# Forgetting bias of odd heads moved to rows 64 to 127 of the array

## The chip, the cores and the metric

The kernel runs on one core of a Trainium2 chip. The metric is the device time of one execution in microseconds (us), the median of several runs.

## What is computed

Two requests go through a hybrid encoder of two layers: a prompt of 256 tokens and a sample step of 32 tokens with 512 cached keys. A layer is a SwiGLU block, one wide projection that feeds three groups of heads (forgetting attention, RWKV-7, retention), an output projection, a second SwiGLU block and a gated embedding. The change concerns the forgetting attention, 8 heads of width 64. Cut to what matters:

```
def fox_block(q, k, v, cq, ck, mask):
    s = jnp.einsum('bqhd,bkhd->bhqk', q, k).astype(F32) * (HEAD_DIM ** -0.5)
    s = s + jnp.swapaxes(cq, 1, 2)[:, :, :, None] - jnp.swapaxes(ck, 1, 2)[:, :, None, :]
    s = jnp.where(mask[None, None], s, -jnp.inf)
    p = jax.nn.softmax(s, axis=-1).astype(v.dtype)
    return jnp.einsum('bhqk,bkhd->bqhd', p, v)
```

Here `cq` and `ck` are running sums of the log forget gates `logf`, per head and token. For the prompt the function is called once for each half of the 256 queries, for the sample with all 512 + 32 keys.

## The kernel before

Everything is written by hand for each engine, with semaphores between them; each engine runs its own instructions in the order of the code. Tokens lie along the free dimension (256 of the prompt, then 32 of the sample), features along the partitions. Two neighbouring heads 2p and 2p+1 form a pair: the even head's 64 features are partitions 0 to 63 of block p of `zT`, the odd head's are partitions 64 to 127.

The bias is made by TensorE. `foxL` (stationary side, 8 heads x 256 prompt columns, then 2 x 128 sample columns) and `foxR` (moving side, 256 + 512 + 32 columns) are all zeros but for rows 0 to 7 and 32 to 39, one row for each head. Rows 0 to 7 of `foxR` are ones and those of `foxL` the query sums; rows 32 to 39 of `foxR` are the key sums and those of `foxL` constants. A product over all 128 rows thus adds the bias to the scores in PSUM, and the query-key product over 64 rows is accumulated on top of it.

The rows are filled during the projection (`z_block` on TensorE, L1486; `z_next` on VectorE, which evicts a block, L931, and makes the low part of the next weights, L922): three scans L1049, L1050, L1052, a copy into `foxR` L1054, then L1056 and L1059 into `foxL`. The rest was zeroed or loaded once at the start (L354, L358 to L361).

The attention itself, once in each layer, is a chain between engines. On TensorE: `scores(0)` between the two calls of `head_sums` (L1752), then in a loop over p `scores(p + 1)`, the transposes of the softmax of pair p (L1804) and the products with the values (L1812). In `scores`, L1776 is the bias, four matmuls with 128, 256, 128 and 256 columns, and L1781 the query-key product, four matmuls with the same columns. VectorE takes the maximum (L1217) and divides by the sum (L1239 to L1241), ScalarE takes exp (L705) and copies the transposes (L712), VectorE gates the output (L1232). GpSimd meanwhile finishes the RWKV output (L460 to L466). Then comes the sample: bias L1823 (512 and 32 columns, twice), scores L1829 (64 rows x 32 columns of the array each), on VectorE the maximum and the softmax (L1278 to L1287), with L1265 and L1272 of the output projection among them, transposes L1840 and L1842, products with the cached values L1848 and L1850, and the output projection L1866.

An fp32 matmul stands in the trace as two records.

Of the kernel before, what the change touches and what calls it, by code (L numbers as in the profile page):

```python
# [79 lines left out]
for _name, _n in (("n1", DB), ("nm", DB), ("n2", DB), ("pn", DB), ("mu", 7), ("prev", 7), ("bf", 1), ("w0", 2),  # L80
# [22 lines left out]
    rsd=10, ro_ps=6, ro_ok=6, rgate=2, fu_ok=1, fl_ok=1, lgf_ok=1, fc_ok=3, vt_ps=3, vtc=3, fs_ps=8, fmx=16,  # L103
# [20 lines left out]
def program(nc, wcol, x_in, p_in, consts_in, params_in, foxl_in, kc_in, vc_in, clf_in, srwkv_in, sret_in,  # L124
            nf_in, y_out, k_out, v_out, logf_out, shift_out, rwkv_out, ret_out):
    with ExitStack() as ctx:
# [210 lines left out]
        with nc.Block() as block:  # L337
            @block.sync
            def _(sp):
# [14 lines left out]
                sp.dma_start(foxL[32:40, :], foxl_in).then_inc(start_sem, 16)  # L354

            @block.gpsimd
            def _(pool):
                pool.memset(foxL[:], 0.0).then_inc(clear_sem, 1)  # L358
                pool.memset(foxR[:], 0.0).then_inc(clear_sem, 1)
                pool.wait_ge(clear_sem, 2)  # L360
                pool.memset(foxR[0:8, :], 1.0).then_inc(clear_sem, 1)  # L361
# [10 lines left out]
        with nc.Block() as block:  # L372
# [100 lines left out]
            def _(act):  # L473
                n_chain = [0]
                for layer in range(DEPTH):
# [87 lines left out]
                    if layer == 0:  # L563
                        act.wait_ge(start_sem, 64)
# [239 lines left out]
            def _(dve):  # L804
                n_chain = [0]
                for layer in range(DEPTH):
# [106 lines left out]
                    if layer == 0:  # L913
                        dve.wait_ge(start_sem, 64)
# [126 lines left out]
                    for b in range(2):  # L1041
# [12 lines left out]
                    link(dve.tensor_copy(foxR[32:40, :], cbuf[e8, :]))  # L1054
                    z_next(22)
                    dve.tensor_tensor(foxLp[e8], cbuf[e8, 0:TP].unsqueeze(1).to_broadcast([8, FOX_H, TP]),  # L1056
                                      w.unsqueeze(2).to_broadcast([8, FOX_H, TP]), ALU.mult).then_inc(S["fc_ok"], 1)
                    for g in range(2):
                        dve.tensor_tensor(foxLs[e8, 128 * g:128 * g + 128].rearrange("p (b t) -> p b t", b=4),  # L1059
                                          cbuf[e8, TP + PAST:].unsqueeze(1).to_broadcast([8, 4, TS]),  # L1060
                                          w.rearrange("p (b g) -> p g b", g=2)[:, g, :].unsqueeze(2).to_broadcast([8, 4, TS]),
                                          ALU.mult).then_inc(S["fc_ok"], 1)
# [300 lines left out]
            def _(pe):  # L1363
                for layer in range(DEPTH):
# [107 lines left out]
                    if layer == 0:  # L1472
                        pe.wait_ge(start_sem, 64)
# [293 lines left out]
                    pe.wait_ge(S["fc_ok"], past["fc_ok"] + 3)  # L1767

                    def scores(p):
# [357 lines left out]
```

## Time and profile before

| | |
|---|---|
| median of 3 runs | 1533.01 us (1532.35 to 1534.19) |
| profiled execution | 1533.06 us, span 1531.2 us |
| granted TensorE clock over the span | 0.944 |
| TensorE matmul busy | 1445.7 us (94%) |
| VectorE busy | 936.0 us (61%) |
| ScalarE busy | 597.0 us (39%) |

Time outside the span is 1.9 us. The span is that from the first to the last instruction. A granted clock of 1.00 is 2.4 GHz and 0.50 is 1.2 GHz; times within a layer are given as us from the start of the span.

### The profile page before, as it was taken

To read this page: it belongs to the slowest core of one execution; us is meant where nothing else is said; L and a number is where in the kernel's file an instruction comes from. 1 tells how busy PE (TensorE), PEld (TensorE's weight loads), DVE (VectorE), ACT (ScalarE), POOL (GpSimd) and SP (SyncE) were. 2 spreads that over 40 slices of the span, in tenths; PEclk is the share of its full clock that TensorE was granted. 3 is DMA by queue.
4 is the path that set the end of the run, shared out by engine and by line. 5 is a ranking of instruction groups with operands and counts; after the bars stand their busy time and mean duration, and the time that the engine had idled before them with its cause. 6 is when DMAs were issued, how large, how long until landed. Compare 5 with 4: busy or idle time off the path is not lost.

```text
span 1531.2 us, 26488 instructions
## 1 busy us (share of the span) xinstructions
PE 1445.7 (94%) x11102; PEld 1381.5 (90%) x11102; DVE 936.0 (61%) x1517; ACT 597.0 (39%) x837; POOL 41.4 (3%) x67
## 2 busy tenths in 40 slices
PE   6999998997987999999999999999899789999997
PEld 6999998997766999999989999989787579999997
DVE  5666456867555566663766663579583645666536
ACT  5444343531133544432554442444210435444334
POOL 1000000001020000000000000000100200000000
PEclk9999999998676999999999999999985879999998
DMA  8444443340020444444444444343400123444440
GB/s 322 166 164 165 165 164 110 135 170 32 5 71 30 164 153 165 162 166 162 159 164 163 164 164 164 122 147 138 158 1 12 64 83 138 167 165 164 165 163 32
DMA packets 31318, 205.47 MB, mean 134 GB/s; under 512 B 4312, under 2 KB 5864, under 8 KB 7544
## 3 DMA queue, kind: packets, MB, share of 16 engines
q1 hardware_dynamic: 28672, 195.98, 35.3%
q0 software_dynamic: 2560, 8.26, 1.5%
q8 instruction: 64, 1.05, 0.3%
q14 instruction: 22, 0.18, 0.0%
HBM read 200.13 MB, written 4.10 MB: 133 GB/s over the span
## 4 chain that ended last, share of the span: by engine, by line
PE 87%; DVE 7%; ACT 3%; issue 2%; DMA 0%; SPq 0%; DVEq 0%; ACTq 0%
PE bank L1411 37%; PE bank L1434 18%; PE bank L1486 10%; PE bank L1903 3%; PE bank L1866 3%; PE bank L1594 1%; PE bank L1601 1%; PE bank L1871 1%; PE bank L1848 1%; PE bank L1884 1%; PE bank L1606 1%; PE bank L1687 1%; PE bank L1582 1%; PE bank L1717 1%; PE bank L1776 1%
## 5 line engine op out<-in xcount | busy, mean ns | idle before, releaser
L1411 PE MATMUL bank<-split_x,split_w 128*128 128x288 f32 x4224 | 569.4, 297 | 16.2 <-ACT split_x L498 11.8
L1411 PEld LDWEIGHTS bank<-split_x,split_w 128*128 128x128 f32 x4224 | 566.2, 189 | 18.9 <-issue 11.8
L831 DVE TENSOR_TENSOR split_w<-wc,split_w 128x2048 fp32r<-128x2048 f32 x139 | 318.6, 2292 | 343.4 <-ACT split_w L514 343.4
L514 ACT ACTIVATE split_w<-wc 128x2048 fp32r<-128x2048 f32 x139 | 266.4, 1916 | 397.7 <-PE bank L1411 206.2
L1434 PE MATMUL bank<-split_x,split_w 128*128 (+1 forms) x2112 | 282.3, 295 | 0.0
L1434 PEld LDWEIGHTS bank<-split_x,split_w 128*128 128x128 f32 x2112 | 281.8, 188 | 0.0
L1486 PE MATMUL bank<-split_h,split_x 128*128 128x288 f32 x752 | 115.5, 301 | 5.6 <-ACT split_x L572 4.2
L1486 PEld LDWEIGHTS bank<-split_h,split_x 128*128 128x128 f32 x752 | 105.7, 191 | 9.0 <-DVE zT L931 5.1
L572 ACT ACTIVATE split_x<-wc 128x1024 fp32r<-128x1024 f32 x62 | 65.2, 1057 | 112.2 <-PE bank L1486 96.7
L539 ACT ACTIVATE et<-hT 128x288 f32<-128x288 f32 x88 | 35.5, 445 | 110.3 <-DVE hT L850 110.3
L1486 PE MATMUL bank<-split_x 128*128 128x288 f32 x496 | 76.1, 296 | 0.0
L1486 PEld LDWEIGHTS bank<-split_x 128*128 128x128 f32 x496 | 69.5, 189 | 0.0
L1903 PE MATMUL bank<-split_x,split_w 128*128 128x288 f32 x384 | 52.9, 297 | 0.0
L1903 PEld LDWEIGHTS bank<-split_x,split_w 128*128 128x128 f32 x384 | 51.7, 189 | 1.1 <-ACT split_x L771 1.1
L931 DVE TENSOR_TENSOR zT<-bank,rs 128x288 f32<-128x288 f32 x62 | 28.1, 453 | 32.0 <-PE bank L1486 23.1
L1486 PE MATMUL bank<-split_h,split_e 128*128 128x288 f32 x240 | 39.2, 308 | 7.5 <-DVE split_e L922 7.5
L855 DVE SCALAR_TENSOR_TENSOR et<-et,hT 128x288 f32<-128x288 f32 x88 | 36.4, 455 | 12.7 <-ACT et L539 9.1
L922 DVE TENSOR_TENSOR split_x<-wc,split_x 128x1024 fp32r<-128x1024 f32 x32 | 39.0, 1218 | 7.8 <-ACT split_x L572 7.8
L1486 PEld LDWEIGHTS bank<-split_h,split_e 128*128 128x128 f32 x240 | 35.2, 198 | 8.4 <-DVE split_e L922 8.4
L861 DVE SCALAR_TENSOR_TENSOR et<-et,bank 128x288 f32<-128x288 f32 x88 | 39.3, 450 | 4.1 <-PE bank L1411 2.5
L922 DVE TENSOR_TENSOR split_e<-wc,split_x 128x1024 fp32r<-128x1024 f32 x30 | 36.5, 1217 | 6.8 <-ACT split_x L572 6.8
L850 DVE TENSOR_TENSOR hT<-bank,rs 128x288 f32<-128x288 f32 x88 | 35.9, 450 | 5.9 <-ACT rs L493 5.9
(293 smaller groups left out, 1404.7 us busy)
## 6 DMA issues: line engine op xcount, KB each, us to landing
wc<-wcol SPq DMA_DIRECT2D x182, 1024.0 KB, 4.8
con<-consts_in SPq DMA_DIRECT2D x1, 2182.0 KB
arena<-kc_in POOLq DMA_DIRECT2D x8, 256.0 KB, 3.3
arena<-vc_in POOLq DMA_DIRECT2D x2, 1024.0 KB, 5.2
xT<-x_in SPq DMA_DIRECT2D x2, 576.0 KB, 4.3
k_out<-zT POOLq DMA_DIRECT2D x8, 144.0 KB, 2.2
v_out<-zT POOLq DMA_DIRECT2D x8, 144.0 KB, 2.2
y_out<-hT SPq DMA_DIRECT2D x8, 144.0 KB, 1.9
```

Source lines behind the costliest of these rows:

```text
L514: act.activation(ws[(s + 1 - f) % 2][0], wc[:, p % RING, :], ACT.Copy).then_inc(S["cast"], 1)
L572: act.activation(zw[n % 2][0], z_raw(n), ACT.Copy).then_inc(S["zcast"], 1)
L831: dve.tensor_tensor(lo, wc[:, (POS_FFN[f] + s) % RING, :], hi, ALU.subtract).then_inc(S["wlo"], 1)
L850: dve.tensor_tensor(half[:, q % 2, :], bank[2 * (q % 4)][:, 0:T], rs[:], ALU.mult)\
L855: dve.scalar_tensor_tensor(e, e, 1.0, half[:, q % 2, :], ALU.add, ALU.mult)\
L861: dve.scalar_tensor_tensor(e, e, 0.5, bank[2 * (q % 4) + 1][:, 0:T], ALU.mult, ALU.mult)\
L922: dve.tensor_tensor(lo, z_raw(n), hi, ALU.subtract).then_inc(S["zlo"], 1)
L1411: mm = pe.matmul(o, w[:, k, cs], x[:, k, :], start=(n == 0 and k == 0), stop=(n == 2 and k == DB - 1))
L1434: return pe.matmul(bank[m][:, 0:T], w[:, kk, m * 128:m * 128 + 128], rhs, start=start, stop=stop)
L1486: mm = pe.matmul(o, w[:, k, :], zh_lo(k) if second else zh_hi[:, k, :], start=(i == 0 and k == 0), stop=(i == 2 and k == DB - 1))
L1866: pe.matmul(bank[2 * s + cc][:, 0:T], hi[:, k, cc * 128:cc * 128 + 128], x[:, k, :], start=(x is oh_hi and k == 4), stop=False)
L1903: mm = pe.matmul(bank[2 * s + cc][:, 0:T], w[:, k, cc * 128:cc * 128 + 128], x[:, k, :], start=(n == 0 and k == 0), stop=(n == 2 and k == ...
```

## The change

The even heads' biases stay in rows 0 to 7 and 32 to 39, and a second set is written in rows 64 to 71 and 96 to 103. `foxL` gets the query sums of even heads in rows 0 to 7 alone, those of odd heads in rows 64 to 71. A bias matmul now reads 64 rows, those of its own head's half, and the bias matmuls of a pair alternate between the halves, as the score matmuls already do. The constants are loaded twice, the ones are set twice, the copy into `foxR` is made twice, and the one multiply of 8 heads becomes two of 4 heads.

```
@@ first block
-                sp.dma_start(foxL[32:40, :], foxl_in).then_inc(start_sem, 16)
+                for row in (32, 96):
+                    sp.dma_start(foxL[row:row + 8, :], foxl_in).then_inc(start_sem, 16)
-                pool.memset(foxR[0:8, :], 1.0).then_inc(clear_sem, 1)
+                for row in (0, 64):
+                    pool.memset(foxR[row:row + 8, :], 1.0).then_inc(clear_sem, 1)
@@ VectorE, during the projection
-                    link(dve.tensor_copy(foxR[32:40, :], cbuf[e8, :]))
+                    for row in (32, 96):
+                        link(dve.tensor_copy(foxR[row:row + 8, :], cbuf[e8, :]))
                     z_next(22)
-                    dve.tensor_tensor(foxLp[e8], cbuf[e8, 0:TP].unsqueeze(1).to_broadcast([8, FOX_H, TP]),
-                                      w.unsqueeze(2).to_broadcast([8, FOX_H, TP]), ALU.mult).then_inc(S["fc_ok"], 1)
                     for g in range(2):
-                        dve.tensor_tensor(foxLs[e8, 128 * g:128 * g + 128].rearrange("p (b t) -> p b t", b=4),
+                        own = slice(64 * g, 64 * g + 8)
+                        mine = w.rearrange("p (b g) -> p g b", g=2)[:, g, :].unsqueeze(2)
+                        dve.tensor_tensor(foxLp[own].rearrange("p (b g) t -> p g b t", g=2)[:, g],
+                                          cbuf[e8, 0:TP].unsqueeze(1).to_broadcast([8, 4, TP]),
+                                          mine.to_broadcast([8, 4, TP]), ALU.mult).then_inc(S["fc_ok"], 1)
+                        dve.tensor_tensor(foxLs[own, 128 * g:128 * g + 128].rearrange("p (b t) -> p b t", b=4),
                                           cbuf[e8, TP + PAST:].unsqueeze(1).to_broadcast([8, 4, TS]),
@@ TensorE, scores
-                        for e in range(2):
-                            for q, k1, at in parts:
-                                pe.matmul(bank[score_bank(2 * p + e)][:, at:at + k1], foxLp[:, 2 * p + e, q:q + 128], foxR[:, 0:k1],
+                        for q, k1, at in parts:
+                            for e in range(2):
+                                hs = slice(64 * e, 64 * e + 64)
+                                pe.matmul(bank[score_bank(2 * p + e)][:, at:at + k1], foxLp[hs, 2 * p + e, q:q + 128], foxR[hs, 0:k1],
                                           start=(at == 0), stop=False, skip_group_check=True)
@@ TensorE, sample
-                    for g in range(2):
-                        for i, (k0, k1) in enumerate(keys):
-                            pe.matmul(bank[2 * g + i][:, 0:k1 - k0], foxLs[:, 128 * g:128 * g + 128], foxR[:, TP + k0:TP + k1],
+                    for i, (k0, k1) in enumerate(keys):
+                        for g in range(2):
+                            hs = slice(64 * g, 64 * g + 64)
+                            pe.matmul(bank[2 * g + i][:, 0:k1 - k0], foxLs[hs, 128 * g:128 * g + 128], foxR[hs, TP + k0:TP + k1],
                                       start=True, stop=False, skip_group_check=True)
```

The waits on `start_sem` and `fc_ok` count the added load (80 for 64) and the added multiply (4 for 3).

On TensorE, `scores(0)` of the first layer stands before as follows (the width is that of output rows x columns, and bank0 and bank1 are the two heads of pair 0):

```order
L1776 MATMUL bank0<-foxR,foxL 128x128
L1776 MATMUL bank0<-foxR,foxL 128x256
L1776 MATMUL bank1<-foxR,foxL 128x128
L1776 MATMUL bank1<-foxR,foxL 128x256
L1781 MATMUL bank0<-zT 128x128
L1781 MATMUL bank1<-zT 128x128
```

and with the change as follows (L1776 is now L1782, L1781 is L1787):

```order
L1782 MATMUL bank0<-foxR,foxL 128x128
L1782 MATMUL bank1<-foxR,foxL 128x128
L1782 MATMUL bank0<-foxR,foxL 128x256
L1782 MATMUL bank1<-foxR,foxL 128x256
L1787 MATMUL bank0<-zT 128x128
L1787 MATMUL bank1<-zT 128x128
```

The number and size of the matmuls are the same; banks 0 and 1 now alternate in the bias too.

On VectorE, the place in the projection where the rows are filled stands before as follows:

```order
L1054 COPY foxR<-extra 8x800
L931 TENSOR_TENSOR zT<-bank,rs 128x288
L922 TENSOR_TENSOR split_x<-wc,split_x 128x1024
L1056 TENSOR_TENSOR foxL<-extra,con 8x2048
L1059 TENSOR_TENSOR foxL<-extra,con 8x128 x2
L931 TENSOR_TENSOR zT<-bank,rs 128x288
```

and with the change as follows (L931 is now L933, L922 is L924):

```order
L1057 COPY foxR<-extra 8x800 x2
L933 TENSOR_TENSOR zT<-bank,rs 128x288
L924 TENSOR_TENSOR split_x<-wc,split_x 128x1024
L1062 TENSOR_TENSOR foxL<-extra,con 8x4x256
L1065 TENSOR_TENSOR foxL<-extra,con 8x128
L1062 TENSOR_TENSOR foxL<-extra,con 8x4x256
L1065 TENSOR_TENSOR foxL<-extra,con 8x128
L933 TENSOR_TENSOR zT<-bank,rs 128x288
```

One copy is added ahead of one block's eviction, and the multiply of 2048 elements is two of 1024.

## Rows read from the trace of the kernel before

**Rows 1.** Page, chain that ended last: share of the span by engine.

```profile
PE 87%; DVE 7%; ACT 3%; issue 2%; DMA 0%; SPq 0%; DVEq 0%; ACTq 0%
```

**Rows 2.** Chain in order of time, first layer's attention: start, us, what.

```profile
440.38 1.31 PE bank L1776 x8
441.69 0.86 PE bank L1781 x8
...
446.00 1.46 DVE arena L1240
...
447.49 1.51 DVE arena L1241
...
452.42 2.54 PE bank L1776 x8
454.96 0.91 PE bank L1781 x8
455.87 0.28 DVE bank L1217
...
468.99 3.57 PE bank L1823 x8
472.56 1.26 PE bank L1829 x29
...
477.02 0.64 PE bank L1840 x4
```

**Rows 3.** The same chain in the second layer, sample bias.

```profile
1223.25 3.61 PE bank L1823 x8
```

**Rows 4.** Timeline, GpSimd and VectorE between the first two pairs.

```profile
445.97 1.40 POOL L464 TENSOR_TENSOR arena<-arena 128x576 f32<-128x576 f32 x1
446.00 1.45 DVE L1240 TENSOR_SCALAR arena<-arena 128x128 f32<-128x128 f32 x1
...
447.45 1.40 POOL L466 TENSOR_TENSOR hT<-arena 128x576 f32<-128x576 f32 x1
447.49 1.51 DVE L1241 TENSOR_SCALAR arena<-arena 128x256 f32<-128x256 f32 x1
...
449.11 0.28 DVE L1240 TENSOR_SCALAR arena<-arena 128x128 f32<-128x128 f32 x1
```

**Rows 5.** Stretches: length, busy us (count) of PE, PEld, DVE, ACT, POOL, then clock.

```profile
447.70:451.00 3.30, 1.13 (x8) 0.66 (x8) 3.23 (x12) 1.07 (x3) 1.15 (x1) 1.00 0.00 0
451.10:454.40 3.30, 3.30 (x15) 2.43 (x14) 1.78 (x7) 1.42 (x8) 0.00 (x0) 0.50 0.00 0
468.20:471.50 3.30, 3.30 (x11) 1.79 (x8) 2.42 (x3) 2.03 (x2) 0.00 (x0) 0.50 0.00 0
471.60:475.00 3.40, 2.04 (x36) 0.87 (x34) 1.78 (x6) 0.17 (x1) 0.00 (x0) 1.00 0.47 140
478.50:492.00 13.50, 12.88 (x88) 11.37 (x89) 1.89 (x7) 2.05 (x8) 0.00 (x0) 0.50 0.00 1
```

**Rows 6.** Timeline, TensorE, output projection's first matmuls.

```profile
491.15 6.45 PE L1866 MATMUL bank<-split_x,split_w 128*128 128x288 f32 x32
```

**Rows 7.** Timeline, VectorE and TensorE in the first layer's projection.

```profile
308.42 0.57 DVE L1054 COPY foxR<-extra 8x800 f32<-8x800 f32 x1
...
310.53 2.27 DVE L1056 TENSOR_TENSOR foxL<-extra,con 8x2048 f32<-8x2048 f32 x1
...
317.31 1.21 DVE L922 TENSOR_TENSOR split_x<-wc,split_x 128x1024 fp32r<-128x1024 f32 x1
...
319.32 1.23 PE L1486 MATMUL bank<-split_h,split_x 128*128 128x288 f32 x8
...
321.07 0.94 DVE L1070 TENSOR_TENSOR et<-bank,con 128x288 f32<-128x288 f32 x2 [2.55 <-PE bank L1499]
```

**Rows 8.** Timeline, the end of the first block.

```profile
5.97 2.77 ACT L369 ACTIVATE hT<-xT 128x288 f32<-128x288 f32 x8 [3.94 <-DMA xT<-x_in]
6.57 0.38 SPq L354 DMA_DIRECT2D foxL<-foxl_in x1
```

More of the change, by code:

```diff
@@ L102 @@
     gn_ps=8, gn_sq=2, gn_ln=4, gn_rs=2, rot_ps=4, rotd=4, decd=2, rtr_ps=3, rtrc=3, sm_ps=6, smd=6, kv_ps=5,
-    rsd=10, ro_ps=6, ro_ok=6, rgate=2, fu_ok=1, fl_ok=1, lgf_ok=1, fc_ok=3, vt_ps=3, vtc=3, fs_ps=8, fmx=16,
+    rsd=10, ro_ps=6, ro_ok=6, rgate=2, fu_ok=1, fl_ok=1, lgf_ok=1, fc_ok=4, vt_ps=3, vtc=3, fs_ps=8, fmx=16,
     fexp=16, fpn=8, ft_ps=8, ftc=8, fo_ps=8, fo_ok=8, ss_ps=2, smx=2, sexp=4, spn=2, st_ps=4, stc=4, so_ps=2,
@@ L563, in _ @@
                     if layer == 0:
-                        act.wait_ge(start_sem, 64)
+                        act.wait_ge(start_sem, 80)
                     def z_cast(n):
@@ L913, in _ @@
                     if layer == 0:
-                        dve.wait_ge(start_sem, 64)
+                        dve.wait_ge(start_sem, 80)
                     def z_rest(n):
@@ L1053, in _ @@
                                                 cbuf[e8, TP + PAST - 1:TP + PAST], ALU.mult, ALU.add))
-                    link(dve.tensor_copy(foxR[32:40, :], cbuf[e8, :]))
+                    for row in (32, 96):
+                        link(dve.tensor_copy(foxR[row:row + 8, :], cbuf[e8, :]))
                     z_next(22)
-                    dve.tensor_tensor(foxLp[e8], cbuf[e8, 0:TP].unsqueeze(1).to_broadcast([8, FOX_H, TP]),
-                                      w.unsqueeze(2).to_broadcast([8, FOX_H, TP]), ALU.mult).then_inc(S["fc_ok"], 1)
                     for g in range(2):
-                        dve.tensor_tensor(foxLs[e8, 128 * g:128 * g + 128].rearrange("p (b t) -> p b t", b=4),
+                        own = slice(64 * g, 64 * g + 8)
[4 more added lines that the diff above has]
+                        dve.tensor_tensor(foxLs[own, 128 * g:128 * g + 128].rearrange("p (b t) -> p b t", b=4),
                                           cbuf[e8, TP + PAST:].unsqueeze(1).to_broadcast([8, 4, TS]),
-                                          w.rearrange("p (b g) -> p g b", g=2)[:, g, :].unsqueeze(2).to_broadcast([8, 4, TS]),
-                                          ALU.mult).then_inc(S["fc_ok"], 1)
+                                          mine.to_broadcast([8, 4, TS]), ALU.mult).then_inc(S["fc_ok"], 1)
                     z_next(23)
@@ L1472, in _ @@
                     if layer == 0:
-                        pe.wait_ge(start_sem, 64)
+                        pe.wait_ge(start_sem, 80)
                     def z_block(n):
@@ L1766, in _ @@
                         mm.then_inc(S["vt_ps"], 1)
-                    pe.wait_ge(S["fc_ok"], past["fc_ok"] + 3)
+                    pe.wait_ge(S["fc_ok"], past["fc_ok"] + 4)
                     def scores(p):
```

## Prediction

> **What bounds the kernel now.** I read the page first: TensorE carries 87% of the chain that ended last, VectorE and ScalarE 10% [rows 1]. So I looked at the chain in order of time around the changed lines. In the projection, where the bias rows are written, the chain is almost all TensorE. In the attention it jumps between engines: the bias and the scores of pair 0, then ScalarE and VectorE, then L1776 and L1781 of pair 2, then VectorE from 455.87 on, and at the end the sample's bias L1823 and scores L1829 [rows 2]. The biases of pairs 1 and 3 are missing from it: TensorE runs them while it would wait for VectorE in any case. The second layer's chain has the same pieces, its sample bias 3.61 us [rows 3], so I work out the first layer and count it twice.
>
> Three readings carry the argument. The reader should first compare the bias with the scores of the same pair: both are 8 records with the same columns, yet the bias takes 1.31 us of chain and the scores, whose heads use separate halves of the rows, 0.86 us [rows 2]. Second, the same bias takes 2.54 us for pair 2 [rows 2], because in that stretch the granted clock is 0.50; it was 0.50 under the sample's bias as well and 1.00 after both [rows 5]. Third, VectorE's two divisions for pair 0 take 1.45 and 1.51 us, while the next one of the first kind takes 0.28; each of the long ones ends right after a GpSimd operation that started just before it (445.97 + 1.40 = 447.37 against 447.45, and 448.85 against 449.00) [rows 4].
>
> **The biases, size by size.** Before, the four bias matmuls of a pair follow one another. With the change two run side by side, each over half of the rows and into its own bank. The price of such a group lies between half of 1.31 us, 0.66, and what the score group takes, 0.86 [rows 2]. The difference of 0.20 us is what a group pays for starting after a matmul over all rows. The bias now pays it, but the scores right behind it, which stay in the same halves, no longer do: together 1.31 + 0.86 = 2.17 us become about 0.86 + 0.66 = 1.52. I take a saving of 0.65 us at clock 1.00; the lower bound is 0.45. At clock 0.50 the saving doubles.
>
> The Trainium skill, TensorEngine Tiling (Tiling Modes, Key Properties), states that a change of the tiling mode drains the engine and that its two row tiles work in parallel. By "up to 2x" for a side of at most 64, the bias alone would save 0.66 us; if every group paid the drain, only 0.45. The trace shows both effects in the 0.86.
>
> **Pair 0 to pair 2.** Scores(0) ends 0.65 us earlier, and with it the exps of pair 0 and the start of VectorE's division at 446.00, now about 445.35. GpSimd's work does not hang on it and stays. By the pattern of [rows 4] the first division then ends before L464 instead of behind it, the second behind L464 (447.5 instead of 449.0), but the division of the pair's other head behind L466, about 0.5 us earlier than before (its start was 449.11). So 0.5 us of the 0.65 reach the transposes. The bias of pair 1 also gets shorter, at no gain: behind it TensorE only waits longer for VectorE, with 1.13 us of work in the 3.30 us from 447.7 on [rows 5]. That longer wait may cost something, which is the second rival.
>
> Pair 2's bias, 2.54 us at clock 0.50, and its scores, 0.91 us, end at 455.87 [rows 2]. Side by side, the bias takes 1.3 us at this clock. If the clock returns at the same moment, near 454.5 (it was 0.50 up to 454.4, [rows 5]), the scores now run mostly before it, at the low clock, 1.3 us instead of 0.66. From a start between 451.9 and 452.4 (the 0.5 us earlier, less what the values lose where they too meet the low clock), this ends by 455.0. From there VectorE is the limit: its divisions of pair 1 are done at about 455.0 as before, since they wait for the values of pair 0. The gain is thus 0.85 us at 455.87, and it is carried through VectorE's chain up to the sample's bias. Pair 3's bias is hidden under that chain.
>
> **The sample.** L1823 takes 3.57 us [rows 2], all but its end at clock 0.50 [rows 5]. Halved and with a start like that above it takes about 2.0 at the low clock: 1.6 us saved. But the clock returned at about 471.5, and L1829, 1.26 us at clock 1.00, would now start at 470.1 rather than 472.56. Most of it runs at the low clock, as 0.6 to 0.8 us more. That leaves 0.85 + 1.6 - 0.7 = 1.75 us. Then TensorE waits for VectorE's softmax. It had 2.04 us of work in the stretch from 471.6 [rows 5]; of that, about 0.4 is left after 471.6, so I expect the clock to fall sooner than 478.4, and L1840 (0.64 us at 477.02) to cost 0.45 more. The small products of the cached values ran at clock 0.50 before (12.88 us busy in 478.5 to 492.0) and do after: 1.3 us left. The output projection, dense work, started at 491.15 [rows 6] at the low clock. Starting 1.3 us earlier, it gains that in full only if the clock returns that much earlier too. If it returns at the same moment, half of the 1.3 is left, 0.65; if the earlier start makes it return much sooner, say by the 3.4 us for which it stayed low around pair 2 (451.1 to 454.5, [rows 5]), it is 1.3 / 2 + 3.4 / 2 = 2.35. I take 1.7 us, between the two and a little over the 1.3.
>
> **What is added.** On VectorE one copy of 0.57 us and one more multiply, whose 2.27 us for 2048 elements become two of about 1.2 (like the 1024 columns of L922, 1.21): about 0.65 us in all in each layer [rows 7]. Behind it wait the evictions and weight splits for TensorE. The closest is L922, which ends at 318.52 and is wanted at 319.32: 0.80 us of slack, 0.15 left. Next VectorE waits 2.55 us for TensorE at 321.07, where all lateness ends. Cost nothing; without that cover 0.65 a layer, 1.3 in all. The second load of constants (0.38 us to issue, from 6.95 on) and the second small memset lie ahead of ScalarE's end of the first block, 8.74 [rows 8]: nothing.
>
> **Sum.** 2 x 1.7 = 3.4 us. The profiled execution took 1533.06 (span 1531.2 and 1.9 around it), 0.05 above the median of 1533.01: 1533.0 - 3.4 = **1529.6 us**. 0.2% of it, 3.07 us, is about what a measurement of this kernel can tell from no change.
>
> **Rivals.**
> (1) *The clock eats it.* With less work between its waits, TensorE falls to clock 0.50 sooner. For: it fell at 451.1 after 1.13 us of work in 3.30, and pair 1's shorter bias leaves the stretch before that one with about as little. Transposes and values of pair 0 then run at the low clock throughout and push pair 2's start 0.3 to 0.5 us beyond the 452.4 assumed above; the values of pair 2 (0.65 us) may follow; and if the output projection's clock returns late, only 0.65 of the first gain counts: 0.3 to 1.2 us a layer, 1530.6 to 1532.4, about 1531.5. Against: both bias savings on the chain lie in stretches that are at 0.50 anyway. The Trainium skill, TensorE: Matmul & The Clock Gate (HAM oscillation), warns that idle gaps between bursts throttle the clock again; by that rule this rival's 1531.5 holds, and the trace agrees as far as the fall at 451.1 goes.
> (2) *All of it arrives.* The clock stays up or returns sooner at 454.5, 471.5 and in the output projection: 2.5 to 3.2 us a layer, 1526.6 to 1528.0, about 1527.3.
> (3) *Slower: the clock does not come back at 454.5.* It returned after a stretch in which TensorE was busy throughout, 3.30 of 3.30 [rows 5], with the biases over all rows. If records over half the rows don't raise it, scores(2) end at 455.3, and up to the sample the transposes (0.33 us each, twice), the values (0.65, twice) and pair 3's 1.5 us run at half speed. That costs about 3 us, part of it under VectorE's chain, less the 1.7, so 1.3 a layer and 2.6 in all, and with the same at 471.5 (L1829 and L1840, 0.6 a layer) 3.8: about 1536. It decides from 3.2 us of lost clock a layer. Against: after L1781's records over halves the clock stayed at 1.00.
> (4) *The halves don't overlap*: the bias stays at 1.31 us and the time at 1533 within 0.5. Against: L1781 does it in this trace with the same columns and banks.
>
> **How the numbers follow.** Chances: forecast (gain 2.2 to 5) 0.62, rival 1 0.22, rival 2 0.08, rival 3 0.05, rival 4 0.03. Faster by over 0.2% are rival 2 and some 0.45 of the forecast's 0.62, since its middle lies just beyond the bound: 0.53. Slower is rival 3: 0.05. The rest, 0.42, is within 0.2%. The range: down to 1527.4 leaves out most of rival 2, up to 1531.9 takes in rival 1 up to where its gain is 1.1; outside lie about 0.06 and 0.12.
>
> **What would show it.** Right: the bias group of 8 records at about 0.7 to 0.9 us at clock 1.00, records of a pair starting together; L1823's successor near 2.0 us or less; pair 2's maximum on VectorE 0.8 to 0.9 us earlier counted from scores(0); no new wait of TensorE near 319 and 1073. Wrong: a clock of 0.50 before 451 or over pair 3; the output projection starting earlier while its clock returns at the old distance; and above all a clock that is up longer than I allow.

## The result, and the profile after

The changed kernel took **1539.91 us** (median of 10 executions, 1533.17 to 1541.94), the kernel before 1534.28 beside it (10 executions, 1532.35 to 1537.47). The ratio is 1.0027, 95% interval 1.0016 to 1.0038: slower by a quarter of a per cent, 4 us by the ratio and 5.6 by the medians, where 1529.6 was forecast and 1527.4 to 1531.9 given as the range. The profiled execution took 1535.9, with a span of 1534.3 and a mean granted clock of 0.935, against 0.944 before. It is thus the second quickest of the ten, and some of the loss has to be looked for in other profiles. Of all executions in this text one was slow, 1602.56 us at a granted clock of 0.814, one of the eight of the changed kernel with pair 1's bias twice and no fillers; its ratio leaves it out.

The page's chain by engine reads as in [rows 1], to the per cent. The chain in order of time, in the first layer's attention, answers to [rows 2]:

```profile
441.05 0.86 PE bank L1782 x8
441.91 0.66 PE bank L1787 x8
...
446.02 0.30 DVE arena L1245
...
446.34 0.40 DVE arena L1246
...
446.84 1.33 DVE arena L1245
...
448.20 1.52 DVE arena L1246
...
452.79 1.58 PE bank L1782 x8
454.37 1.15 PE bank L1787 x8
455.52 0.28 DVE bank L1222
...
469.31 2.28 PE bank L1830 x8
471.59 1.59 PE bank L1836 x32
...
476.38 1.10 PE bank L1847 x4
```

Read the third column first. The bias took 1.31 us and takes 0.86, its scores took 0.86 and take 0.66: the price of changing between whole and half rows has moved to the group in front, as worked out. Pair 2's bias went from 2.54 to 1.58, the sample's from 3.57 to 2.28. But now the first column: the chain enters at 441.05 instead of 440.38, 0.67 late, and VectorE's maximum L1222, which was at 455.87, is at 455.52. Behind the sample's bias the gain shrinks again: L1836 takes 1.59 instead of 1.26 and L1847 1.10 instead of 0.64.

The stretches of [rows 5], with the granted clock third from the right:

```profile
447.70:451.00 3.30, 0.90 (x3) 0.50 (x3) 3.24 (x10) 0.47 (x2) 1.77 (x2) 0.59 0.04 17
451.10:454.40 3.30, 3.16 (x20) 2.27 (x22) 1.45 (x5) 1.70 (x9) 0.00 (x0) 0.50 0.00 0
468.20:471.50 3.30, 3.30 (x16) 1.66 (x12) 2.10 (x3) 2.36 (x2) 0.00 (x0) 0.50 0.01 2
471.60:475.00 3.40, 1.37 (x32) 0.40 (x32) 2.74 (x6) 0.81 (x3) 0.00 (x0) 0.91 0.35 104
478.50:492.00 13.50, 12.88 (x89) 11.38 (x89) 1.65 (x6) 2.05 (x8) 0.00 (x0) 0.50 0.01 1
```

In the first row the clock was 1.00 and is 0.59: it falls 2.8 us sooner than before (448.3 against 451.1). That is outside the forecast and inside rival 1.

The preparation [rows 7] is no longer covered. The timeline, VectorE and TensorE:

```profile
318.70 1.22 DVE L924 TENSOR_TENSOR split_x<-wc,split_x 128x1024 fp32r<-128x1024 f32 x1
...
319.98 1.32 PE L1491 MATMUL bank<-split_h,split_x 128*128 128x288 f32 x8
...
321.82 0.94 DVE L1075 TENSOR_TENSOR et<-bank,con 128x288 f32<-128x288 f32 x2 [1.90 <-PE bank L1504]
```

TensorE's group started at 319.32 and starts at 319.98, right behind VectorE's L924. It waited 0.23 us for it. When I match the two kernels matmul for matmul, the changed one is 0.49 us late ahead of this group and 0.75 behind it, so 0.26 us come from here. The rest is from the start: its first matmul of all is at 12.13 instead of 11.81. Over all the profiles of this text that moment lies between 11.6 and 12.5 with the added load and between 11.6 and 12.0 without it, so these 0.3 us may be no more than spread.

All that is small, and with the shorter attention it sums to almost nothing: 0.2 us late at 520. Where the span's 3 us went is seen far from any edited line, in TensorE's wait between the two layers. Stretches of the kernel before:

```profile
766.40:769.80 3.40, 0.46 (x4) 0.22 (x2) 3.30 (x8) 1.09 (x3) 0.00 (x0) 1.00 0.48 154
769.80:773.20 3.40, 2.94 (x21) 2.72 (x22) 1.50 (x5) 3.37 (x4) 1.64 (x3) 1.00 0.52 198
773.20:776.60 3.40, 3.40 (x28) 3.40 (x27) 2.29 (x1) 0.77 (x2) 0.00 (x0) 1.00 0.00 0
```

and of the changed one:

```profile
766.40:769.80 3.40, 0.46 (x5) 0.22 (x3) 3.29 (x8) 1.03 (x4) 0.00 (x0) 0.91 0.42 140
769.80:773.20 3.40, 3.15 (x11) 2.83 (x12) 1.66 (x5) 3.37 (x4) 1.63 (x3) 0.50 0.54 212
773.20:776.60 3.40, 3.40 (x18) 3.40 (x18) 2.29 (x1) 0.62 (x1) 0.00 (x0) 0.59 0.00 0
```

The work and the wait are the same; TensorE idles 2.94 us for ScalarE there in both. The matmuls that end this wait and the one in the second layer's projections, before and then after:

```profile
769.63 0.40 PE L1411 MATMUL bank<-split_x,split_w 128*128 128x288 f32 x1 [2.94 <-ACT split_x L779]
990.92 1.28 PE L1486 MATMUL bank<-split_h,split_x 128*128 128x288 f32 x8 [2.10 <-ACT split_x L572]
```

```profile
769.79 0.61 PE L1416 MATMUL bank<-split_x,split_w 128*128 128x288 f32 x1 [2.94 <-ACT split_x L781]
993.44 1.40 PE L1491 MATMUL bank<-split_h,split_x 128*128 128x288 f32 x8 [2.10 <-ACT split_x L574]
```

Before, the clock stayed up. After, it is 0.50 from 769.2 to 776.0, and in the second and third stretch 29 matmuls are done where 49 were. The same happens from 994.5 to 997.9, behind the wait of 2.10 us. Matmul for matmul, the changed kernel is 0.2 us late at 764 and 2.5 at 780; 2.5 late at 988 and 3.9 at 1000. The two falls cost 2.4 and 1.4 us.

### The profile page after: what moved, and what is told of

It reads as the page before. It is cut to its first block, busy times and chain, and to the rows that moved or that the text cites. A ratio compares the mean times of both kernels' runs of the same rounds, so it can differ in the third digit from the quotient of the medians.

```text
span 1534.3 us, 26494 instructions
## 1 busy us (share of the span) xinstructions
PE 1445.0 (94%) x11102; PEld 1381.7 (90%) x11102; DVE 937.8 (61%) x1521; ACT 596.9 (39%) x837; POOL 42.1 (3%) x68
## 4 chain that ended last, share of the span: by engine, by line
PE 87%; DVE 7%; ACT 3%; issue 2%; DMA 0%; SPq 0%; DVEq 0%; ACTq 0%
PE bank L1416 37%; PE bank L1439 18%; PE bank L1491 10%; PE bank L1910 3%; PE bank L1873 3%; PE bank L1599 1%; PE bank L1606 1%; PE bank L1878 1%; PE bank L1855 1%; PE bank L1891 1%; PE bank L1611 1%; PE bank L1692 1%; PE bank L1587 1%; PE bank L1818 1%; PE bank L1722 1%
## 5 line engine op out<-in xcount | busy, mean ns | idle before, releaser
L933 DVE TENSOR_TENSOR zT<-bank,rs 128x288 f32<-128x288 f32 x62 | 28.1, 454 | 33.6 <-PE bank L1491 24.6
L924 DVE TENSOR_TENSOR split_x<-wc,split_x 128x1024 fp32r<-128x1024 f32 x32 | 39.0, 1217 | 7.8 <-ACT split_x L574 7.8
L924 DVE TENSOR_TENSOR split_e<-wc,split_x 128x1024 fp32r<-128x1024 f32 x30 | 36.5, 1218 | 6.8 <-ACT split_x L574 6.8
```

The source lines that it names most:

```text
L924: dve.tensor_tensor(lo, z_raw(n), hi, ALU.subtract).then_inc(S["zlo"], 1)
```

## The experiments

Three theories stood at first. **A**: the loss comes from TensorE's waits outside the attention, where a shift of some tenths of a us decides whether the clock falls. **B**: the halves in the attention cost the time themselves. **C**: the preparation does. In each job the kernel before ran beside the others: 1534.07, 1534.82, 1534.07, 1533.94 and 1535.69 in the five jobs. Ratios are against it. Where I subtract medians of different jobs, the ratios give about 1 us less.

**The kernel before once more**, no edit.

> The kernel before, unchanged, for a second profile and more times. Theory A (the clock outside the attention: TensorE has fixed pauses between the layers and in the projection, and whether the clock falls to 0.50 in them varies from execution to execution): times spread over 1532 to 1538, and the profile shows a stretch at 0.50 near 767 to 776 or near 990 to 998 if its time is above 1534. Theory B (the cost is in the attention): the profile repeats the attention's low stretches of the first profile (8 low stretches of 3.4 us between 447 and 496 less those at 1.00) and the time is within 1 us of 1533.

1534.25, ratio 1.0003 (0.9992 to 1.0013), profiled span 1531.2. The clock's pattern is that of the first profile.

**The changed kernel once more**, no edit.

> The changed kernel, unchanged. Theory A: in the profile the attention (from the first bias to the end of the first slice of the output projection) is 0.5 to 1 us shorter in each layer than in the kernel before, and all that its time is above 1533 shows as stretches at clock 0.50 elsewhere. Theory B: the attention is 1 to 3 us longer in each layer than before, with more time at 0.50 in it. Theory C (the added work of VectorE and of the start): 0.3 us at the start and 0.3 us in each projection, 1 us in all, and no more. Times 1533 to 1542, median 1538 to 1540 by all of them.

1539.79, ratio 1.0030 (1.0018 to 1.0043), profiled span 1541.2, clock 0.930: the loss is real and this profile is a slow example, 10 us above that of the kernel before. It shows the falls near 770 and 995 again, and a second kind of loss: ahead of the attention of each layer, while TensorE is busy without a pause, the clock comes back late, at 441.4 instead of 434.1 in the first layer. A stretch of the kernel before, and of this run:

```profile
434.10:437.40 3.30, 3.30 (x44) 2.67 (x41) 2.34 (x8) 0.00 (x0) 0.51 (x1) 1.00 0.00 0
```

```profile
434.10:437.40 3.30, 3.30 (x41) 2.73 (x38) 1.73 (x6) 0.00 (x0) 0.00 (x0) 0.50 0.02 5
```

Matmul for matmul that costs 3.1 us in the first layer (0.6 late at 425, 3.7 at the attention's first bias) and 3.2 in the second (7.4 at 1178, 10.5 at the first bias). With 2.2 and 1.5 for the two waits, they make up all of the 10 us; what start and preparation add, 0.8 in all, the two attentions nearly give back (0.65).

**The preparation alone.** The added load, memset, copy and multiply, with the matmuls of before over all rows.

```
-link(dve.tensor_copy(foxR[32:40, :], cbuf[e8, :]))
+for row in (32, 64):
+    link(dve.tensor_copy(foxR[row:row + 8, :], cbuf[e8, :]))
...
+own = slice(0, 8)
```

> All of the change's added work (second load, second memset, second copy, two multiplies for one) but the bias matmuls over all 128 rows in the old order; the second copy goes to rows 64 to 71, where the stationary side is zero. Theory C: plus 1 us over the kernel before, 0.3 at the start and 0.3 in each layer at the matmuls near 319 and 1073. If the preparation is the whole cost: plus 4 us. Theory A: plus 1 us from the shares above and a spread as wide as that of the other kernels. Theory B: plus 0 to 1 us, and a spread like that of the kernel before.

1534.19, ratio 1.0006 (0.9995 to 1.0017), no fall near 770 or 995. C is out as a cause of the whole, to within 2.6 us.

**Only the prompt in halves**: the sample's bias goes over all rows, as before.

```
-    for i, (k0, k1) in enumerate(keys):
-        for g in range(2):
-            hs = slice(64 * g, 64 * g + 64)
-            pe.matmul(bank[2 * g + i][:, 0:k1 - k0], foxLs[hs, ...], foxR[hs, ...],
+    for g in range(2):
+        for i, (k0, k1) in enumerate(keys):
+            pe.matmul(bank[2 * g + i][:, 0:k1 - k0], foxLs[:, ...], foxR[:, ...],
```

> The change for the prompt's biases alone; the sample's bias stays a product over 128 rows (its constants are loaded into rows 32 to 39 only). Theory B with the prompt as its cause: as slow as the changed kernel, plus 3 to 5 us over before. Theory B with the sample as its cause: plus 0 to 1 us. Theory A: the attention is 0.3 to 0.9 us shorter than before in each layer by the profile, the sample's bias takes 3.6 us again if the clock is low there, and the time lies anywhere from 0 to plus 5 us with the stretches at 0.50 outside the attention.

1538.5, ratio 1.0035 (1.0022 to 1.0047). The prompt's part is enough for the loss; the falls near 770 and 995 are there.

**Shifting the wait.** Six needless matmuls in the changed kernel's first output projection, ten in that of the kernel before, to move all that follows by 0.8 and 1.3 us.

```
+again = 6 if (layer, s, cc, k) == (0, 1, 0, 4) and x is oh_hi else 0
+for r in range(1 + again):
     pe.matmul(bank[2 * s + cc][:, 0:T], hi[:, k, ...], x[:, k, :],
```

> The changed kernel with 6 needless matmuls of 0.133 us (0.8 us) in the first layer's output projection, after the clock has returned; they write what the next one overwrites. Theory A (the halves end the attention earlier, and TensorE's fixed pause between the layers, 2.9 us, then lies so that the clock falls in it; it fell 2.2 to 2.5 us after the pause began in three profiles with halves, and not in three with whole rows): the pause is moved by 0.8 us against the moments at which the clock changes, there is no stretch at 0.50 near 769 and none near 994, and the time goes down from 1539 to 1534 to 1536 although work is added. Theory B (the halves themselves cost time, in the attention or by what they do to the engine): 1539.8 plus 0.8, 1540.6.

> The kernel before with 10 needless matmuls of 0.133 us (1.33 us) at the same place in the first layer. Theory A: the pause between the layers, which the clock just survives in the kernel before, now lies so that most of it falls into what follows the next such moment: a stretch at 0.50 near 770 to 776, and the time rises by 1.3 and 2 to 4 more, to 1537 to 1540. Theory B: 1534.1 plus 1.3, 1535.4.

The first took 1540.43, 1.0025 (1.0009 to 1.0041): no better than the changed kernel, and the clock still fell, near 775 and 997. The hope that the shift would mend it failed. The second took 1537.68, 1.0023 (1.0013 to 1.0032): 2.9 us more than the kernel before, of which 1.3 are the added work. Its profile has falls at 774 and 996 which the kernel before has not, and a late return ahead of the second attention. That speaks for A: a loss of the same kind, 1.6 us, without any edit in the attention.

**Filling the waits.** Two fillers: 18 needless matmuls in the wait between the layers, and four in each layer behind the third block's projections, in the wait of 2.10 us.

```
+if layer and f == 0 and begin and s == 0 and q == 0 and n == 0 and k == 6:
+    for r in range(3):
+        for j in range(6):
+            pe.matmul(o, w[:, j, cs], x[:, j, :], start=(j == 0), stop=(j == 5 and r < 2))
...
+pe.wait_ge(S["z_ev"], past["z_ev"] + 3)
+for _ in range(4):
+    pe.matmul(bank[2][:, 0:T], c("ident"), c("cos"), start=True, stop=True)
```

> The changed kernel with TensorE's pauses filled: 18 needless matmuls (2.4 us) in the 2.9 us pause between the layers, and 4 of 0.49 us in each layer's 2.1 us pause after the first norm in the projection (near 234 and 988). They lie in waits, so they cost nothing by themselves. Theory A: no stretch at 0.50 near 769 or 994, time 1534 to 1535.5. Theory B: no gain, 1539 to 1540.

> The kernel before with the same fillers. Theory A: the same profile as before in the attention, no stretch at 0.50 near 237, 769 or 994 in any execution, so a narrower spread and a median 0 to 1.5 us below that of before; the kernel with halves and fillers is then 0 to 1 us faster or slower than this one, by 0.5 to 0.7 us of gain in each attention less 1 us of preparation. Theory B: 1534, and the kernel with halves and fillers 4 to 5 us slower than this one.

The changed kernel took 1531.85 with both, 0.9987 (0.9977 to 0.9997); the kernel before 1533.82, 0.9996 (0.9988 to 1.0005). The needless work takes 8 us off the one (6.6 by the ratios) and nothing measurable off the other. The changed kernel is now 2.0 us the faster by the medians, though the two intervals overlap a little; B, by which it had to stay 4 us the slower, falls. TensorE in the wait between the layers, timeline of the first:

```profile
765.32 0.96 PE L1420 MATMUL bank<-split_x,split_w 128*128 128x288 f32 x6
766.12 2.56 PE L1417 MATMUL bank<-split_x,split_w 128*128 128x288 f32 x18
769.24 0.40 PE L1420 MATMUL bank<-split_x,split_w 128*128 128x288 f32 x1 [0.56 <-ACT split_x L781]
```

The wait of 2.94 us is 0.56; the clock does not fall, and nothing waits for the 18.

**Each filler alone**, in the changed kernel.

> The changed kernel with only the first of the two fillers: 18 needless matmuls in TensorE's wait between the layers (near 766 to 770). Theory A (the clock falls in this wait and in the one after the first norm, and that alone makes the change slower): the stretch at clock 0.50 that began at 769 and 772 in the profiles of the changed kernel is gone; since the other one (994 to 998) also depended on where its wait lay, it may go with it or stay. Against the changed kernel's 1539.8: about 2.5 us less if only the first goes, 1537.3; about 4 us less if both go, 1535.8; more than 5.5 us less (below 1534.5) only if the rises before the attention come back too. Theory B (the attention in halves itself costs the time): no change, 1539.8, and the stretches in the attention as before.

> The changed kernel with only the second filler: four needless matmuls behind the third block of projections in each layer, where TensorE waits after the first norm's weights (near 234 and 991). Theory A: the stretch at clock 0.50 near 994 to 998 is gone (1.6 us), the one at 769 to 772 stays: about 1538.2, between the changed kernel's 1539.8 and the one with both fillers, 1531.9. If this filler instead carries most of the 8 us, its effect is on where the later stretches lie (the rise before the attention, missed in two of four profiles of the changed kernel), and the time is below 1535. Theory B: no change, 1539.8.

Between the layers: 1533.4, 0.9993 (0.9983 to 1.0004). After the norm: 1536.09, 1.0013 (1.0003 to 1.0023). The first gives back 6.4 us, far more than the 2.2 to 2.4 that its own stretch is worth, the second 3.7, against 1.4 to 1.5. Their profiles keep one fall each, the first at 989 for 3.4 us, the second at 770, and have the late return ahead of the first layer's attention alone. So a filler also changes what the clock does where it adds nothing, and the sizes can't be laid to single stretches.

**A third filler**, 16 matmuls in each layer's wait of 2.2 us for the weights of the tenth block (near 261 and 1016), on both kernels; and the changed one of them once more in another job.

```
+if n == 9 and i == 1:
+    for r in range(16):
+        pe.matmul(o, hi[:, r % DB, :], (zh_lo(r % DB) if r >= DB else zh_hi[:, r, :]),
+                  start=(r == 0), stop=False)
```

> The changed kernel with both fillers, and a third: 16 needless matmuls in each layer where TensorE waits for the weights of the tenth block of projections (near 261 to 263.4 and 1015 to 1018), the wait in which the clock also fell in most profiles of the kernel before. Theory A: the single stretches at 263 and at 1018 are gone, worth about 1.7 us each when the matmuls behind them are dense: 1528.5 against 1531.9 with two fillers. A rival: the matmuls are longer than the wait for the weights at the high clock and only put off the work behind them: 1532 to 1534, no better than two fillers.

> The kernel before with the same three fillers. With the clock's falls outside the attention out of both kernels, the difference between this one and the changed kernel with three fillers is what the change itself is worth: by the profiles, 0.5 to 0.7 us in the attention of each layer, less about 0.3 us of uncovered preparation in each layer: the changed kernel 0.5 to 1.5 us faster. Time: 1530.4 if the third filler saves 1.7 us a layer (1533.8 with two fillers), 1533.8 or more by the rival. Theory B: the changed kernel is slower here too, by 4 us or more (with two fillers it was 2.0 us faster).

> The changed kernel with three fillers once more, as the control for the three beside it: 1528.2, within 1.0. By its last profile the first layer's clock is 0.50 from about 448 to 454.5, for two steps in a row where the kernel before has one.

Changed kernel: 1528.15, 0.9958 (0.9942 to 0.9974), and 1527.88, 0.9950 (0.9934 to 0.9966). Kernel before: 1529.16, 0.9971 (0.9958 to 0.9984). With the falls in these waits gone from both, the change is worth about 1 us, with intervals that overlap. The late return is still there: the changed kernel's two profiles (spans 1527.4 and 1526.2) have it in the first layer, the kernel before (1524.9) in none.

**Inside the attention.** The forecast was 1.7 us a layer, and the profiles show less. The distance from the attention's first bias matmul to the output projection's first product with the low part of the weights is the same within 0.4 us in every profile of a kind, wherever in the span it lies. So I read there when the clock was 0.50, in us after that first matmul (worked out from the trace's record of the granted clock, first layer; the distances are of both layers):

| kernels | clock 0.50 from : to | distance, us |
|---|---|---|
| kernel before | 10.88:14.30, 24.54:31.36, 38.19:55.26 | 57.2, 57.2 |
| changed | 7.34:14.17, 21.00:31.24, 34.65:55.13 | 56.6, 56.5 |
| changed, three fillers (second job) | 7.43:14.25, 21.08:31.32, 34.73:55.21 | 56.7, 56.5 |

Each of the three falls comes 3.4 us sooner after the change, and each return at the same distance as before. (In the second layer the second fall does so in three of eight profiles with both parts in halves; in the other five it stays at 24.4 to 24.5.) In the second profile of the changed kernel the distances are 56.8 and 56.9, so the gain is 0.3 to 0.7 us a layer. What was hidden work before, the bias of pair 1, is now 0.6 us shorter, and TensorE waits longer for VectorE around it. The transposes of pair 0's second head, before and then after:

```profile
449.83 0.55 PE L1804 MATMUL bank<-con,arena 128*128 128x128 f32 x3 [0.23 <-DVE arena L1241]
```

```profile
449.76 0.90 PE L1810 MATMUL bank<-con,arena 128*128 128x128 f32 x3 [2.42 <-DVE arena L1246]
```

The first head's waited 2.25 us and wait 0.80. Theory **A2**: that shorter work lets the clock fall sooner. **B2**: the wait itself does.

**The bias of pair 1 twice**, so that TensorE is busy as long as before, and nothing waits for it.

```
-for q, k1, at in parts:
+for q, k1, at in parts + (parts if p == 1 else ()):
```

> As the control, but the bias of pair 1, which nothing waits for, is issued twice, so that TensorE is busy there about as long as before the change. Theory A2 (that hidden work kept the clock up): the stretch at clock 0.50 begins one step later, near 451, and lasts one step instead of two; the transposes and values of pair 0 run partly at clock 1.00, pair 2's bias starts 0.3 to 0.8 us sooner after the bias of pair 0, and the time is 0.5 to 1.5 us a layer less than the control's, 1525.2 to 1527.2. Theory B2 (the clock falls there because of the long wait for VectorE's divisions, whatever stands before it): still two steps from 448, and the control's time within 0.5.

1523.85, 0.9933 (0.9915 to 0.9950): 4.0 us less than the same kernel without the repetition in this job, 1527.88, for eight records more a layer. By the ratios it is 2.6 us, and with six executions of each the intervals overlap (four of the six are below all six of the other); the traces are the clearer evidence. Timeline of TensorE without and then with the repetition:

```profile
445.43 0.55 PE L1822 MATMUL bank<-con,arena 128*128 128x128 f32 x3 [0.80 <-DVE arena L1246]
448.38 0.90 PE L1822 MATMUL bank<-con,arena 128*128 128x128 f32 x3 [2.41 <-DVE arena L1246]
449.87 1.55 PE L1830 MATMUL bank<-arena,extra 128*64 128x256 f32 x8 [0.58 <-ACT arena L714]
451.34 1.65 PE L1794 MATMUL bank<-foxR,foxL 64*128 64x128 f32 x8
```

```profile
443.59 0.55 PE L1822 MATMUL bank<-con,arena 128*128 128x128 f32 x3 [0.15 <-DVE arena L1246]
446.55 0.55 PE L1822 MATMUL bank<-con,arena 128*128 128x128 f32 x3 [2.41 <-DVE arena L1246]
447.68 0.87 PE L1830 MATMUL bank<-arena,extra 128*64 128x256 f32 x8 [0.58 <-ACT arena L714]
448.48 0.93 PE L1794 MATMUL bank<-foxR,foxL 64*128 64x128 f32 x8
```

The same wait of 2.41 us stands in both, so B2, by which the wait alone brings the fall, does not hold. The wait in front of it went from 0.80 to 0.15, and the same transposes, values and bias now take 0.55, 0.87 and 0.93 instead of 0.90, 1.55 and 1.65. The clock is not 0.50 there at all in the first layer; in the second from 11.02 to 14.43, as in the kernel before. The last stretch ends at 52.1 and 52.0 instead of 55.2, and the distance is 53.8 and 53.9.

**Filling the wait that follows**: eight matmuls before the transposes of pair 0's second head.

```
+if h == 1:
+    for _ in range(8):
+        pe.matmul(bank[4][:, 0:T], c("ident"), c("cos"), start=True, stop=True)
```

> As the control, with eight needless matmuls (about 2.2 us) before the transposes of pair 0's second head, in TensorE's 2.4 us wait for VectorE. Theory A2 and B2 alike: the clock stays at 1.00 until 451 or beyond. If it stays up through pair 2, its bias and scores take 0.86 + 0.66 instead of 1.58 + 1.27 us and the values of pair 0 0.87 instead of 1.55: VectorE is then the limit at 455 and at most 1 us a layer is gained, 1526.2. If the fall only moves into pair 2's bias and scores or to pair 3, nothing is gained: 1528.2 or a little more.

1536.02, 1.0014 (1.0000 to 1.0028), 8 us more than without them. I had put them behind the instruction that waits for VectorE, not ahead of it: they start at 447.61 after the same 2.41 us and take 7.05 us at the low clock. It tests neither theory.

**The sample's bias over all rows again**, on the kernel with three fillers (the edit of the prompt-only kernel above).

> As the control, but the sample's bias goes over all 128 rows again, as before the change. By the profiles the halves save 3.57 - 2.28 = 1.3 us in that group and lose 0.3 in the scores behind it and 0.45 in the next transposes, since the clock returns at the same moment: 0.5 us a layer net, so 1.0 us slower than the control, 1529.2. If the whole 1.3 us a layer were kept: 1530.8. If nothing of it reaches the end: 1528.2.

1530.66, 0.9973 (0.9960 to 0.9986): 2.8 above the kernel with both parts in halves by the medians, with single executions from 1526.8 to 1534.9 around both. The distance is 57.1 and 57.1 instead of 56.7 and 56.5: 0.4 to 0.6 us a layer, so the expected 0.5 by the profile. The rest of the 2.8 I can't place.

**The repetition alone**, without fillers, and on the kernel before with three.

> The changed kernel, without any filler, with the bias of pair 1 issued twice. By theory A2, from the first bias of the attention to the first low-weight product of the output projection it takes about 53.9 us in each layer instead of 56.6, so 5.3 us less than the changed kernel's 1539.8 in all if the falls elsewhere stay as they are: 1534.5. The later waits shift by 2.7 us and more, so the falls near 770 and 994 may come or go: 1530.5 to 1536. If the repetition only works together with the fillers: 56.6 us a layer and 1539.8.

> The kernel before with three fillers and the bias of pair 1 issued twice, over all rows, 2.6 us of work instead of 1.3 in a wait of 4.3 us. If the gain is the repetition's alone, the stretch at clock 0.50 at 451 goes, pair 2's bias takes 1.31 instead of 2.8 us, and the attention is 2 to 3 us a layer shorter here too: 1524 to 1525 against 1529.2. If the clock falls there by the wait itself, its place moves by at most one step and the time is 1529.2, or up to 1 us more a layer where the repetition holds up the transposes of pair 0.

The first took 1531.07, 0.9967 (0.9954 to 0.9981): against the ratio of the changed kernel in the first of these jobs, 1.0030, that is 9.7 us less, by one line. The distance is 53.7 and 54.3, and the clock is 0.50 from 10.86 to 14.27 in both layers, as in the kernel before. That is 5.1 us. The other 4.6 are not explained: the falls at 767 and 993 are still there, and the late return is there in both layers. The second took 1527.62, 0.9955 (0.9941 to 0.9969), 2.4 us less than without the repetition by the ratios, intervals overlapping; its distance is unchanged at 57.3 and 57.2, its first fall at 11.0. So the repetition brings nothing inside the attention of the kernel before: there the clock falls where it fell without it. The gain in the attention belongs to halves and repetition together.

The best of all is the changed kernel with three fillers and the repetition, 1523.85: 0.67% under the kernel before. With the one line alone it is 0.33%.

## Why the prediction was wrong

**The biases, size by size: right.** 0.86 + 0.66 = 1.52 us for pair 0, as forecast; 1.58 for pair 2 where 1.3 was forecast, which lies between twice 0.66 and twice 0.86, as if a group behind whole rows paid for the start at the low clock too; 2.28 for the sample where 2.0 was.

**Pair 0 to pair 2: right in sum, otherwise in its parts.** In the first layer both divisions of the first head are now short and both of the second head long. GpSimd meanwhile:

```profile
445.29 1.30 POOL L464 TENSOR_SCALAR arena<-arena,par 128x288 f32<-128x288 f32 x2
446.68 1.40 POOL L466 TENSOR_TENSOR arena<-arena 128x576 f32<-128x576 f32 x1
```

The short ones, 446.02 to 446.74, run beside its TENSOR_SCALAR, the long ones beside its two TENSOR_TENSOR. So it is not GpSimd's work as such that holds VectorE up here, which the reading of [rows 4] left open. Pair 2's bias starts 11.74 us after that of pair 0 instead of 12.04, 0.3 sooner and not 0.5: the transposes of the second head start 0.84 sooner, but at clock 0.50 they take 0.90 instead of 0.55, and the values 1.55 instead of 1.46. Its maximum comes 14.47 us after that bias instead of 15.49 ([rows 2] and the chain above): 1.0 gained, against 0.85 forecast.

**Up to the sample: a loss not foreseen.** I let the 0.85 be carried up to the sample's bias. It starts 28.26 us after the first instead of 28.61, so 0.65 of the 1.0 is lost on the way, where the second fall comes 3.4 us sooner. In the second layer, without that, 0.9 arrives. **Around the sample: right in kind, 0.4 us too high in the first layer and 0.2 in the second.** L1829's loss is 0.33 and, in the second layer, 0.63 (0.6 to 0.8 forecast), L1840's 0.46 in both (0.45). The sample's transposes are 1.3 us nearer to the first bias than before, in the second layer 1.5 (1.75 forecast).

**The output projection: failed.** I took 1.7 between 0.65, for a clock that returns at the same moment, and 2.35. The output projection starts 0.95 us sooner after the first bias (49.99 against 50.94), and its clock returns at 55.1 to 55.4 after that bias where it was 55.2 to 55.3, in all sixteen attentions of the eight profiles with both parts in halves and no repetition. So the gain is 0.6 and 0.7 (0.4 and 0.3 in the second profile): at most my lower bound, the end for a clock that returns at the same moment. I named that end and chose against it; it makes 2.1 to 2.7 us of the miss in both layers together.

**The preparation: failed by its small slack.** 0.65 against 0.80 of slack was counted as hidden, and the term put at nothing; it cost 0.26 to 0.29 us a layer at the group behind, 0.5 in all. "Where all lateness ends" was wrong: TensorE itself was late by then, and nothing behind gives it back.

**Rival 1 was right inside the attention.** "Pair 1's shorter bias leaves the stretch with about as little" work: the clock fell 3.4 us sooner, in every such profile, and the gain of 0.3 to 0.7 us a layer lies in the rival's 0.3 to 1.2. What the sooner falls take was underrated all the same: with that work restored the attention is 2.2 to 2.9 us a layer shorter still, more than the forecast's whole 1.7. The rival's 1531.5 for the kernel was missed for what lies outside the attention. The Trainium skill, TensorE: Matmul & The Clock Gate (HAM oscillation), warns of idle between bursts; the traces agree only in part: the idle of 2.41 us stood both with a fall at 7.4 us and without, and what differed was 0.65 us of idle in front of it.

**What made it slower was in no rival, and is the step that failed most.** The sum took everything outside the attention as standing still but for the preparation. Rival 3, the slower one, looked for its price in a clock that stays low behind pair 2; it came back there at 14.2 us, as before (14.3). In the runs, the clock in the wait between the layers and after the third block's projections cost 2.2 to 2.4 and 1.4 to 1.5 us, and the late return of the second profile 3.1 to 3.2 a layer. That the first two waits carry the loss is shown by the fillers: with two, the changed kernel is 8 us faster by the medians and the kernel before is not. How the 8 us are shared out is not shown, since each filler alone gives back more than its own fall is worth.

**What stays open** is the late return. In all profiles the clock comes back either 5.8 to 6.3 us ahead of the attention's first bias or 2.6 to 2.9. It is the late one in 1 of 12 attentions of kernels without the added preparation, and in 14 of 28 of kernels with it, in both layers of the preparation-only one too. That one still took no longer: its clock was 0.50 for 51.2 us in all between 355 and the first attention, as in the kernel before, because it had come back sooner from the fall at 355. The second profile of the changed kernel has 58.0 there, in both layers, and so has its copy shifted by 0.8; all others have 51.2 or 44.4. So the preparation can be what shifts the pattern, but it is not enough for the loss, and a late return does not tell the loss without that sum. Why the late return follows in one execution and not in the next was not tried by itself.

## What to carry over

Before costing an edit that shortens or delays TensorE, list its waits of 2 to 3 us over the whole kernel and ask of each whether the clock is up through it now: a shift of 0.3 us can turn that into 2 us, far away. Work that nothing waits for may be what keeps the clock up; when it is shortened, put the matmuls back, ahead of the wait and not behind it. And compare two versions with such waits filled in both, and read the attention from its own first instruction, or the clock's chance is taken for the change's effect.

## What the runs showed of the hardware

- Where in an attention the clock falls and returns is repeatable: those that occur keep their distance to its first matmul within 0.4 us in all kernels of a kind, though the first layer's begins anywhere from 436.8 to 444.0. It is not the waits that set these moments. Within each of the 20 profiles all falls and returns (without the end of the last low stretch) keep one even spacing, to 0.001 us, across every wait. TensorE's first matmul lies anywhere between two such moments (0.6 to 3.0 us behind one), the attention's first bias 2.4 to 2.9 us behind one in all 40 attentions. So the kernel comes to lie against the clock's moments, not they against it.
- A small delay can grow far away: the changed kernel enters the second layer's attention 4.1 us late (1198.73 against 1194.59), of which 0.2 stood at the first attention's end and 3.8 come from the two falls.
- Needless matmuls in three waits bring the changed kernel to 0.42 to 0.50% under the kernel before, and the kernel before itself 0.29% down.
- In all profiles VectorE's division of 128x128 takes 0.29 us alone, 0.29 to 0.53 beside a GpSimd TENSOR_SCALAR and 1.30 to 1.45 beside a GpSimd TENSOR_TENSOR, the one of 128x256 0.35 alone and 1.50 to 1.52 beside a TENSOR_TENSOR.
